# Six matmuls of a row block: by halves of the tokens in place of by weights

## The chip, the cores and the metric

The kernel runs on one core of a Trainium2 chip. The metric is the device time of one execution in microseconds, as the median of several runs. TensorE multiplies, ScalarE, VectorE and GpSimd work beside it, and SP issues most of the DMAs.

## What is computed

Two layers of a streaming encoder, for 512 prompt tokens and 32 sample tokens with shared weights (544 tokens, 1024 features). All of it is float32. Cut to what matters here, each layer is

```python
# even layer: gated DeltaNet heads and forgetting attention; odd layer: sliding-window attention
xp = xp + ab_mixer(rmsnorm(xp, g_mix), ...)          # or c_mixer
mk, mv = mem_kv(mem_prompt, g_mem, w_xkv)            # 256 memory tokens @ w_xkv
xp = xp + cross_attend(rmsnorm(xp, g_cross), mk, mv, w_xq, w_xo)
xp = xp + sq_relu_mlp(rmsnorm(xp, g_mlp), w_up, w_down)

def sq_relu_mlp(h, w_up, w_down):
    return jnp.square(jax.nn.relu(h @ w_up)) @ w_down   # 1024 -> 4096 -> 1024
```

and the same for xs. Nearly all the arithmetic lies in the products of a 1024-row input with a weight matrix: the input projections, the output projections, the queries and keys of the cross-attention, and above all the two MLPs.

## The kernel before

**Products in two parts.** Every factor of a large product is split into a high part and a low part that TensorE reads as fp32r: the weights into wh (ScalarE's copy, line 1588) and wl (GpSimd's difference, line 722), the activations into xh and xl (or hh and hl in the MLP, mh and ml for the memory tokens, y_split for the output of the first layer's heads). A product is the sum of three: wh with the high part, wh with the low part, wl with the high part.

**Tiles.** A product works through its weights in panels of 256 columns (2048 numbers in each partition), alternately in slot 0 and slot 1 of stage, wh and wl. A panel gives two tiles of 128 output features. A tile needs eight blocks, one for each 128 rows of the weights (k, "row block"); in the product behind the cross-attention, with 512 input rows, a panel has four tiles of four blocks. The 544 tokens are moved in two halves of 272, TOKENS, since a bank of PSUM holds 512 numbers in a partition. The tensor LP has four banks, and the tiles take them by turns: one fills banks 0 and 1 (half 0, half 1), the next banks 2 and 3. These pairs are the slots that block's first argument names. So a block is six matmuls: three pairs of parts, two halves.

**Order.** The function block (line 826) issues one block, and the loop at line 829 runs over the three pairs of parts outside and over the halves inside; line 831 is the matmul. pair (line 836) calls it for two panels. Where the input is only just being made, pair interleaves the first two tiles and waits ahead of each block: ready(i) for the activations' low part, low_ready for the quarter of wl that the block needs (line 852). The first matmul of a tile waits for the slot to be free (wait_free). The last matmul of a tile raises product_done. Then one instruction of ScalarE or VectorE reads both halves of the slot: relu at line 2005 or the scaled copy at line 2539 in the MLP.

**Products with another order.** The memory product uses the same block with a single half of 256 tokens (halves=((0, MEM),), line 1383 and line 1391), so it writes three matmuls in a row into one bank. In the first layer's output projection, head_parts (line 1327) adds four row blocks of the heads' part to one half at a time, without block: twelve matmuls in a row into one bank, line 1336. The gates' small product at line 1056 has a loop of its own over the parts and the halves.

Of the kernel before, what the change touches and what calls it, by code (L numbers as in the profile page):

```python
# [5 lines left out]
def build_program(nc, t):  # L6
# [44 lines left out]
    p = q = d = 0  # L51
    DRAINED = {}
    for name, panels, tpp in order:
# [3 lines left out]
        p, q, d = p + panels, q + panels * tpp, d + panels * tpp // (2 if name[:3] == "mlp" else 1)  # L57
# [21 lines left out]
    with ctx:  # L79
# [6 lines left out]
        def place(name, shape, dt=f32, at=None):  # L86
            size = 4
            for n in shape[1:]:
                size *= n
            size = (size + 31) // 32 * 32  # L90
            if at is None:
                at = cursor[0]
                cursor[0] += size
            return nc.alloc_sbuf_tensor_at(name, shape, dt, offset=at)
# [8 lines left out]
        wh = [place(f"wh{s}", [128, 2048], f32r) for s in range(2)]  # L103
        wl = [place(f"wl{s}", [128, 2048], f32r) for s in range(2)]
# [718 lines left out]
        def _(pe):  # L823
            TOKENS = ((0, HALF), (HALF, N))

            def block(slot, s, col, k, first, last, kt, halves, X):

                for n_, (w, part) in enumerate(((wh, 0), (wh, 1), (wl, 0))):
                    weights = w[s][:, :].rearrange("p (k n) -> p k n", k=kt)[:, k, col:col + 128]
                    for half, (a, b) in enumerate(halves):  # L830
                        mm = pe.matmul(LP[:, 2 * slot + half, 0:b - a], weights, X[part][k][:, a:b],  # L831
                                       start=(first and n_ == 0), stop=(last and n_ == 2), skip_group_check=True)
                if last:
                    mm.then_inc(product_done, 1)

            def pair(free, Pn, tpp, kt, halves, X, ready, after_first=None, order=None, between=None, halved=False):
# [9 lines left out]
                for s in range(2):  # L846
                    if s and between is not None:
                        between()
                    def low_ready(ks):

                        if not (s == 0 and halved):
                            pe.wait_ge(w_lo, PIECES * (Pn + s) + max(ks) * PIECES // kt + 1)

                    per = max(kt // PIECES, 1)
                    if s == 0 and ready is not None:
                        wait_free(0)
                        for i in range(kt + LAG):
                            if i < kt:
                                ready(i)
                                if i % per == 0:  # L860
                                    low_ready(order[i:i + per])
                                block(0, s, 0, order[i], i == 0, i == kt - 1, kt, halves, X)
                            if i == kt and after_first is not None:
                                after_first()
                            if i == LAG:
                                wait_free(1)
                            if i >= LAG:
                                block(1, s, 128, order[i - LAG], i == LAG, i == kt + LAG - 1, kt, halves, X)
                    for i in range(2 if s == 0 and ready is not None else 0, tpp):
                        tile_n = s * tpp + i  # L870
                        wait_free(tile_n)
                        for k in range(kt):
                            if i == 0 and k % per == 0:
                                low_ready((k,))
                            block(tile_n % 2, s, 128 * i, k, k == 0, k == kt - 1, kt, halves, X)
# [294 lines left out]
            for P, part, at in SUMS:  # L1170
                n_ = H * (part.stop - part.start)
# [1538 lines left out]
```

## Time and profile before

| | |
|---|---|
| median of 3 runs | 1610.47 us (1607.56 to 1611.96) |
| the profiled execution's own time | 1612.56 us |
| its span, first to last instruction | 1609.7 us |
| mean granted TensorE clock | 0.991 |
| TensorE matmul busy | 1568.6 us (97%), 13488 matmuls |
| TensorE weight load busy | 1511.5 us (94%), 13488 loads |
| VectorE / ScalarE / GpSimd busy | 653.1 / 567.3 / 617.1 us |

Busy time is the union of the instructions' times; matmuls overlap one another and the loads, so a row's mean duration is longer than the spacing from one start to the next. The spacing is read from the starts in the timeline.

### The profile page before, as it was taken

The numbers are of one execution on the slowest core, as the hardware profiler recorded it, in microseconds if no ns is written. First come the engines' busy times: TensorE is split into PE (matmuls) and PEld (weight loads), VectorE is DVE, ScalarE is ACT, GpSimd is POOL, SyncE is SP. The second block draws the span as 40 slices with busy tenths as digits, with TensorE's granted clock in tenths as the row PEclk, the third lists the DMA queues.
The fourth block names the chain that finished last, engine by engine and source line by source line (L and its number), as shares of the span: only waits on it lengthen the run. The fifth ranks groups of instructions, "written<-read, shape, count | busy, mean of one in ns | idle before, by whom it ended". The sixth has DMA issues, their size and how long they took to land.

```text
span 1609.7 us, 31744 instructions
## 1 busy us (share of the span) xinstructions
PE 1568.6 (97%) x13488; PEld 1511.5 (94%) x13488; DVE 653.1 (41%) x1224; ACT 567.3 (35%) x999; POOL 617.1 (38%) x513
## 2 busy tenths in 40 slices
PE   8999998999999999999999999999999999999998
PEld 8999977888998999999999998699899999999998
DVE  4484156344434522322223534844254223232244
ACT  5123254334435521312223413844354222131332
POOL 3754201113561353453444442035423444443441
PEclk9999999989999999999999999999999999999999
DMA  5222211003241222222223224013412322223221
GB/s 152 92 79 82 80 55 60 3 2 118 84 158 48 80 79 93 91 79 89 96 79 99 86 79 146 2 54 105 131 31 82 99 79 95 90 79 105 79 79 56
DMA packets 123060, 131.84 MB, mean 82 GB/s; under 512 B 6285, under 2 KB 115122, under 8 KB 122930
## 3 DMA queue, kind: packets, MB, share of 16 engines
q1 hardware_dynamic: 118128, 125.24, 24.2%
q10 hardware_dynamic: 4802, 4.66, 0.9%
q8 instruction: 106, 1.74, 0.4%
q14 instruction: 24, 0.20, 0.0%
HBM read 122.44 MB, written 7.45 MB: 81 GB/s over the span
## 4 chain that ended last, share of the span: by engine, by line
PE 46%; issue 31%; POOL 17%; DVE 3%; ACT 2%; DMA 1%; POOLq 0%; ACTq 0%; DVEq 0%
PE LP L831 37%; POOL wl L722 17%; PE LP L1216 3%; PE MP L982 1%; PE LP L934 1%; DMA stage<-in_w_in_ab 1%; PE MP L1056 0%; PE MP L1200 0%; PE MP L1216 0%; PE MP L1303 0%; ACT probs L1641 0%; PE MP L1073 0%; PE MP L1308 0%; PE MP L1312 0%; PE MP L955 0%
## 5 line engine op out<-in xcount | busy, mean ns | idle before, releaser
L722 POOL TENSOR_TENSOR wl<-stage,wh 128x512 fp32r<-128x512 f32 x428 | 576.8, 1379 | 806.2 <-ACT wh L1588 793.7
L831 PE MATMUL LP<-xh,wh 128*128 128x272 f32 x2112 | 441.6, 290 | 8.2 <-DVE xl L2149 5.3
L831 PE MATMUL LP<-xl,wh 128*128 128x272 f32 x2112 | 436.9, 288 | 0.0
L831 PE MATMUL LP<-xh,wl 128*128 128x272 f32 x2112 | 436.5, 288 | 0.0
L1588 ACT CAST wh<-stage 128x2048 fp32r<-128x2048 f32 x107 | 203.7, 1904 | 443.4 <-PE LP L831 418.1
L831 PEld LDWEIGHTS LP<-xh,wh 128*128 128x128 f32 x2112 | 332.1, 189 | 11.4 <-DVE xl L2149 6.9
L831 PEld LDWEIGHTS LP<-xl,wh 128*128 128x128 f32 x2112 | 332.9, 189 | 0.0
L831 PEld LDWEIGHTS LP<-xh,wl 128*128 128x128 f32 x2112 | 331.0, 189 | 0.0
L831 PE MATMUL LP<-hl,wh 128*128 128x272 f32 x1024 | 211.1, 287 | 0.0
L831 PE MATMUL LP<-hh,wh 128*128 128x272 f32 x1024 | 210.6, 287 | 0.0
L831 PE MATMUL LP<-hh,wl 128*128 128x272 f32 x1024 | 210.5, 287 | 0.0
L831 PEld LDWEIGHTS LP<-hh,wl 128*128 128x128 f32 x1024 | 160.7, 188 | 0.0
L831 PEld LDWEIGHTS LP<-hh,wh 128*128 128x128 f32 x1024 | 160.2, 188 | 0.0
L831 PEld LDWEIGHTS LP<-hl,wh 128*128 128x128 f32 x1024 | 160.1, 188 | 0.0
L2524 DVE TENSOR_TENSOR hsq<-rel 128x544 f32<-128x544 f32 x64 | 51.3, 801 | 261.5 <-ACT rel L2005 254.9
L2539 DVE TENSOR_TENSOR dtmp<-LP,rstd 128x544 f32<-128x544 f32 x64 | 46.4, 725 | 245.4 <-PE LP L831 245.4
L2005 ACT ACTIVATE rel<-LP 128x544 f32<-128x544 f32 x64 | 40.0, 625 | 236.9 <-PE LP L831 236.9
L1613 ACT ACTIVATE sq<-x 128x544 f32<-128x544 f32 x56 | 36.6, 654 | 102.7 <-DVE x L2542 56.2
L805 POOL TENSOR_TENSOR BT<-LT,level 128x256 f32<-128x256 f32 (+1 forms) x24 | 18.4, 779 | 138.2 <-DVE LT L2422 104.8
L2528 DVE TENSOR_TENSOR hl<-hsq,hh 128x544 fp32r<-128x544 f32 x64 | 69.7, 1090 | 2.2
L2149 DVE SCALAR_TENSOR_TENSOR xl<-x,cols,xh 128x544 fp32r<-128x544 f32 x48 | 48.5, 1025 | 40.1 <-ACT xh L1618 38.9
L2142 DVE TENSOR_TENSOR acc<-acc,sq 128x544 f32<-128x544 f32 x49 | 47.1, 962 | 16.7 <-ACT sq L1613 14.8
(415 smaller groups left out, 1675.4 us busy)
## 6 DMA issues: line engine op xcount, KB each, us to landing
stage<-in_w_up SPq DMA_DIRECT2D x32, 1024.0 KB, 5.4
stage<-in_w_down SPq DMA_DIRECT2D x32, 1024.0 KB, 5.2
stage<-in_w_in_ab SPq DMA_DIRECT2D x13, 1024.0 KB, 5.3
stage<-in_w_xkv SPq DMA_DIRECT2D x8, 1024.0 KB, 5.2
stage<-in_w_in_c SPq DMA_DIRECT2D x6, 1024.0 KB, 5.0
stage<-in_w_out_ab SPq DMA_DIRECT2D x4, 1024.0 KB, 9.4
stage<-in_w_xq SPq DMA_DIRECT2D x4, 1024.0 KB, 5.3
stage<-in_w_xo SPq DMA_DIRECT2D x4, 1024.0 KB, 5.2
```

The lines of the kernel that those rows point to most:

```text
L722: pool.tensor_tensor(wl[s][:, part], stage[s][:, part], wh[s][:, part].bitcast(f32), ALU.subtract).then_inc(w_lo, 1)
L805: pool.tensor_tensor(BT[s][0:P, k % 2, :, 0:C], LT[s][0:P, :, 0:C], lower, ALU.mult).then_inc(inv_pool[s], 1)
L831: mm = pe.matmul(LP[:, 2 * slot + half, 0:b - a], weights, X[part][k][:, a:b], start=(first and n_ == 0), stop=(last and n_ == 2), skip_gr ...
L1216: return pe.matmul(out, lhsT, rhs, start=start, stop=stop, skip_group_check=True)
L1588: act.copy(wh[s][:, :], stage[s][:, :]).then_inc(w_hi, 1)
L1613: act.activation(sq[:, k % 2, :], x[:, k, :], ACT.Square).then_inc(sq_ready, 1)
L2005: act.activation(rel[:, k % 2, :].rearrange("p (a n) -> p a n", a=2), LP[:, 2 * (k % 2):2 * (k % 2) + 2, 0:HALF], ACT.Relu).then_inc(relu_ ...
L2142: dve.tensor_tensor(acc[:, :], acc[:, :], sq[:, k % 2, :], ALU.add).then_inc(sq_used, 1)
L2149: dve.scalar_tensor_tensor(out=xl[:, k, :], in0=x[:, k, :], scalar=gain(n_, k), in1=xh[:, k, :].bitcast(f32), op0=ALU.mult, op1=ALU.subtra ...
L2524: dve.tensor_tensor(hsq[:, k % 2, :], rel[:, k % 2, :], rel[:, k % 2, :], ALU.mult).then_inc(hsq_ready, 1)
L2528: dve.tensor_tensor(hl[:, k, :], hsq[:, k % 2, :], hh[:, k, :].bitcast(f32), ALU.subtract).then_inc(h_ready, 1)
L2539: dve.tensor_tensor(two(dtmp[:, k % 2, :]), banks(k), two(rstd[:, :]), ALU.mult).then_inc(drained, 1)
```

## The change

The two loops of block change places. Before, the pairs of parts are outside and the halves inside, so consecutive matmuls share their weights and alternate between the two banks of the slot. After, the halves are outside: three matmuls (wh with high, wh with low, wl with high) go into the bank of half 0, and then three into the bank of half 1. The flags start and stop are set by the same conditions, the last matmul of a tile is the same, and no wait is moved.

```diff
             def block(slot, s, col, k, first, last, kt, halves, X):
 
-                for n_, (w, part) in enumerate(((wh, 0), (wh, 1), (wl, 0))):
-                    weights = w[s][:, :].rearrange("p (k n) -> p k n", k=kt)[:, k, col:col + 128]
-                    for half, (a, b) in enumerate(halves):
+                for half, (a, b) in enumerate(halves):
+                    for n_, (w, part) in enumerate(((wh, 0), (wh, 1), (wl, 0))):
+                        weights = w[s][:, :].rearrange("p (k n) -> p k n", k=kt)[:, k, col:col + 128]
                         mm = pe.matmul(LP[:, 2 * slot + half, 0:b - a], weights, X[part][k][:, a:b],
                                        start=(first and n_ == 0), stop=(last and n_ == 2), skip_group_check=True)
                 if last:
```

## Rows read from the trace of the kernel before

**Rows 1.** The page: span; busy time, share, instructions; shares of the chain by engine.

```profile
span 1609.7 us, 31744 instructions
...
PE 1568.6 (97%) x13488; PEld 1511.5 (94%) x13488; DVE 653.1 (41%) x1224; ACT 567.3 (35%) x999; POOL 617.1 (38%) x513
...
PE 46%; issue 31%; POOL 17%; DVE 3%; ACT 2%; DMA 1%; POOLq 0%; ACTq 0%; DVEq 0%
```

**Rows 2.** The longest piece of the chain that ended last: start us, us, what.

```profile
1220.68 375.61 PE LP L831 x3006
```

**Rows 3.** Waits of TensorE: who waited for whom, us in total, times, longest us.

```profile
PE LP L831 <- DVE xl L2149: 5.3, 6, 2.1
PE LP L831 <- POOL wl L722: 3.1, 7, 0.9
```

**Rows 4.** Groups by line and operation: shapes, xcount, busy us, mean ns, idle before.

```profile
L831 PE MATMUL LP<-xh,wh 128*128 128x272 f32 x2112 | 441.6, 290 | 8.2 <-DVE xl L2149 5.3 <-DVE xl L2219 1.8 <-POOL wl L722 0.9
...
L831 PE MATMUL LP<-hh,wl 128*128 128x272 f32 x1024 | 210.5, 287 | 0.0
...
L831 PEld LDWEIGHTS LP<-xh,wh 128*128 128x128 f32 x2112 | 332.1, 189 | 11.4 <-DVE xl L2149 6.9 <-DVE xl L2219 2.2 <-POOL wl L722 1.1
...
L831 PE MATMUL LP<-y_split,wh 128*128 128x272 f32 x96 | 16.1, 290 | 0.0
...
L831 PE MATMUL LP<-mh,wh 128*128 128x256 f32 x128 | 37.0, 289 | 3.0 <-POOL wl L722 2.2 <-DVE kvT L2495 0.8
...
L831 PE MATMUL LP<-y_split,wl 128*128 128x272 f32 x48 | 9.9, 288 | 0.0
```

**Rows 5.** Timeline of TensorE, 391 to 398 us: start us, us, engine, line, names, shapes, xcount.

```profile
391.77 0.29 PE L1336 MATMUL LP<-y_split,wl 128*128 128x272 f32 x1
...
394.42 0.29 PE L1336 MATMUL LP<-y_split,wl 128*128 128x272 f32 x1
394.54 0.66 PE L831 MATMUL LP<-y_split,wh 128*128 128x272 f32 x4
395.05 0.41 PE L831 MATMUL LP<-y_split,wl 128*128 128x272 f32 x2
...
397.32 0.42 PE L831 MATMUL LP<-y_split,wl 128*128 128x272 f32 x2
```

**Rows 6.** Timeline of TensorE, memory product of the second layer, first and last rows of 46.

```profile
1119.14 0.28 PE L831 MATMUL LP<-mh,wl 128*128 128x256 f32 x1
1119.26 0.28 PE L831 MATMUL LP<-mh,wh 128*128 128x256 f32 x1
...
1124.46 0.27 PE L831 MATMUL LP<-mh,wl 128*128 128x256 f32 x1
```

**Rows 7.** Timeline of TensorE in the MLP, first and last rows of 16.

```profile
1495.83 0.41 PE L831 MATMUL LP<-hh,wh 128*128 128x272 f32 x2
1496.08 0.42 PE L831 MATMUL LP<-hl,wh 128*128 128x272 f32 x2
...
1499.58 0.41 PE L831 MATMUL LP<-hh,wh 128*128 128x272 f32 x2
```

**Rows 8.** Stretches of TensorE: us, busy (xcount), granted clock, DMA share, GB/s.

```profile
18.00:30.00 12.00, 11.51 (x84) 0.86 0.20 17
130.00:200.00 70.00, 69.25 (x557) 0.98 0.25 77
260.00:340.00 80.00, 75.60 (x1251) 0.89 0.10 31
600.00:1600.00 1000.00, 989.60 (x8043) 1.00 0.26 82
1118.00:1125.00 7.00, 6.74 (x58) 1.00 0.60 197
```

**Rows 9.** The page's costliest groups, the readers of the finished tiles in the MLP.

```profile
L2539 DVE TENSOR_TENSOR dtmp<-LP,rstd 128x544 f32<-128x544 f32 x64 | 46.4, 725 | 245.4 <-PE LP L831 245.4
L2005 ACT ACTIVATE rel<-LP 128x544 f32<-128x544 f32 x64 | 40.0, 625 | 236.9 <-PE LP L831 236.9
```

## The prediction

> **What bounds the kernel now.** I read the busy table first: TensorE is busy for 1568.6 us of the 1609.7 us span, and VectorE, ScalarE and GpSimd each for 35% to 41% [rows 1]. So the matmuls set the time, unless their 97% hides waiting. The chain that ended last says that it does not: its longest piece is a single run of 3006 matmuls of line 831, 375.61 us long, without a wait in between [rows 2]. That is 375.61 / 3006 = 124.95 ns from one matmul to the next. By engine the chain names GpSimd for 17% and "issue" for 31% [rows 1], but these are places where the program follows another engine back although TensorE is not idle; the table of TensorE's own waits decides, and it holds little: the two longest entries of line 831 are 5.3 us for the low halves of x and 3.1 us for the low parts of the weights [rows 3].
>
> What is edited is line 831 itself. By the counts of its groups it has 2112 matmuls of each of three kinds on x (xh with wh, xl with wh, xh with wl), 1024 of each of three kinds on h, and 96 and 48 on y_split, each of 272 columns; the rows show one kind of each [rows 4]. That is 3 x 2112 + 3 x 1024 + 144 = 9552 matmuls, or 1592 blocks of six. At 125.0 ns these are 1194 us, three quarters of the span. The matmuls on the memory tokens (128 of each of three kinds, 256 columns) have one half only, so their order stays as it is. Everything hangs on one number: does the 125.0 ns from start to start change when the same six matmuls come in another order?
>
> **What the change does to the order.** Before, one block writes the banks as a b a b a b, with the weights wh wh wh wh wl wl and the tokens of xh, xh, xl, xl, xh, xh. After, it writes a a a b b b, with the weights wh wh wl wh wh wl. Nothing is added or taken away: six matmuls, six weight loads, the same operands, and within each bank the same three sums in the same order. Two things per block differ. First, of six steps from matmul to matmul all six changed the bank, and now two do; four steps in six, 4 x 1592 = 6368 in all, now stay in the bank that the matmul before wrote. Second, of six steps three changed the weights, and now four do, which is 1592 more.
>
> **Step 1: the cost of staying in a bank.** The trace of before has both orders side by side, with one operand (y_split) and one width (272 columns). Line 1336 writes three in a row into one bank, and stays there for four row blocks, twelve matmuls, before it goes to the next bank. The matmuls with wl in its rows start at 391.77 and 394.42 us, and seven triples lie between them [rows 5]: 2.65 us / 21 = 126.2 ns. Directly behind, line 831 works on the same operand with the banks in turn: from 395.05 to 397.32 us there are three blocks, 2.27 us / 18 = 126.1 ns. The stamps have steps of 10 ns, so each mean is good to about 0.5 ns, and the difference is +0.1 ns with bounds of about -0.7 and +0.7. The second witness is the memory product, on the same line 831, three in a row into one bank. From 1119.14 to 1124.46 us there are fifteen triples [rows 6]: 5.32 us / 45 = 118.2 ns at 256 columns. In the MLP, with the banks in turn, 30 matmuls of 272 columns take 1495.83 to 1499.58 us [rows 7]: 125.0 ns. The granted clock is 1.00 at both places [rows 8], the level of 2.4 GHz, so 16 columns less should be 16 / 2.4 = 6.7 ns less, and 125.0 - 6.7 = 118.3 ns. Measured 118.2. Put otherwise, what a matmul takes beyond its columns is 125.0 - 113.3 = 11.7 ns with the banks in turn and 118.2 - 106.7 = 11.5 ns three in a row. So I take 0 ns for a step that stays in its bank, and as bounds -0.2 and +0.1 ns from the two comparisons' own differences: 6368 x (-0.2) = -1.3 us and 6368 x 0.1 = +0.6 us. With the rounding of the stamps in full (0.7 ns) the outer bounds would be -4.5 and +4.5 us.
>
> **Step 2: the cost of changing the weights more often.** Every matmul already has a weight load of its own: the two columns of the busy table both count 13488 [rows 1], and the groups of line 831 have as many loads as matmuls [rows 4]. A load takes 189 ns and a matmul 288 ns, while matmuls start every 125 ns, so loads and matmuls overlap. Could the load of the same weights a second time be cheaper? The memory product changes its weights at two steps in three, as the new order does, against one in two before, and its surplus is 11.5 ns against 11.7. The two differ by one change in six steps, so a change would be priced at 6 x (11.5 - 11.7) = -1.2 ns, with some 1.8 ns either way from the stamps: nothing that can be told from 0. I take 0 for the 1592 further changes, with +0.6 ns each (+1.0 us) and -1.2 ns each (-1.9 us) as bounds. Here the Trainium skill has a rule that speaks against the change: the page "TensorE: Matmul & The Clock Gate", section "Step-by-step: what each phase is for", says that loads and matmuls are separate instructions so that weights can be loaded once and used for many matmuls. By that rule the old order has the better shape, and each further change would cost. In this kernel nothing is loaded once: the trace counts one load for each matmul, and the sum would differ by the bound just given at most.
>
> **Step 3: waits and readers.** The waits for xl (through ready) and for the low weights (low_ready, line 852) stand ahead of a whole block. That wl is now needed by the third matmul and not by the fifth, and xl by the second and not the third, delays nothing. The semaphore of a finished tile still rides on the last matmul, half 1 with wl. Half 0 is complete two matmuls, or 250 ns, earlier than before, but no one can use it: the readers take both halves in one instruction, 128x544 [rows 9]. No wait is added, the queues of SP, GpSimd, ScalarE and VectorE keep their order, and their release times stay. Cost 0 on both sides.
>
> **Sum.** 1609.7 us span + 0 + 0 + 0 = 1609.7 us, and with the 2.9 us around it the profiled execution's 1612.6 us. That execution lies 2.1 us above the median of the runs, 1610.47. I therefore predict 1610.5 us.
>
> **The rivals.**
>
> *Faster: changing the bank costs something.* Of the 125.0 ns, 11.7 are not columns. Were all of that the price of a bank change, 6368 steps would give back 74.5 us, and the kernel would take 1536 us. The memory product speaks against it: with no bank change it has the same surplus. What is left is a small share that the stamps hide. At 1 ns a step it would be -6.4 us, 1604.1 us. It decides from 0.76 ns a step, since 0.3% is 4.8 us and 4.8 / 6368 = 0.76 ns.
>
> *Faster: the clock.* Before 370 us the granted clock drops in places: 0.86 from 18 to 30 us, 0.98 from 130 to 200 us, 0.89 between 260 and 340 us [rows 8]. Only the first two stretches are full of line 831. If turn and turn about of the banks made the clock drop there, the change would bring back 0.14 x 12 + 0.02 x 70 = 3.1 us, 1607.4 us, still within 0.3%. But line 831 runs in the same order at 1.00 from 600 to 1600 us, so the order is not what lowers it. The Trainium skill has that rule, too: in "TensorE: Matmul & The Clock Gate", section "A second HAM failure mode: psum-queue depth-cycling", cycling through the PSUM banks is said to make TensorE pause so often that its clock swings between the two levels. By that rule this kernel should swing all along; the trace does not agree, with 1.00 for a thousand us.
>
> *Slower: a sum has to wait for the one before it in its bank.* A matmul lasts 288 ns by its record and the next starts after 125 ns, so in the new order up to three matmuls on the same addresses are under way at once. If the second had to wait for the first to end, the spacing would be 288 ns on four steps in six: 6368 x 163 ns = 1038 us, 2650 us in all. Line 1336 and the memory product do just this and show nothing of it, so the full price is excluded. What they can't exclude is a small stall that needs something they lack, such as ScalarE and VectorE reading the other two banks at the same time, all along. At 1.5 ns a step: +9.6 us, 1620.1 us. It decides from 0.76 ns a step on, that is, where the mean of a long run rises above 125.5 ns (0.76 x 4 / 6).
>
> **How the numbers follow.** No change, 0.90: 1610.5 us, with the range 1606 to 1615 from the bounds of steps 1 and 2 and the runs of before, which lie between 1607.56 and 1611.96 us. Faster by a bank change's price, 0.04: about 1604. The clock, 0.02: 1607.4, within 0.3%. Slower by a stall in the bank, 0.04: about 1620. The range reaches to the first of the faster cases and part of the way to the slower one: 1604 to 1616. About 0.3% is what a measurement of this kernel can tell from no change; so faster 0.04, within 0.3% 0.92, slower 0.04.
>
> **What would show it.** In the profile of after: 13488 loads and 13488 matmuls; in the MLP, twelve matmuls of line 831 in 1.50 us, as now; the memory product at 118 ns, since it is untouched; the readers' 128x544 at their old durations; TensorE busy for about 1569 us, its waits of the same size and at the same places; the granted clock at 1.00 from 600 to 1600 us. The prediction is wrong if the long piece of line 831 has a mean outside 124.5 to 125.5 ns, if fewer weight loads appear (then repeated weights are dealt with in a way that this trace does not show), or if the waits for ScalarE, VectorE or GpSimd grow, which I expect from no step.

## The result and the profile after

The median goes from 1610.47 us (five runs, 1604.11 to 1611.96) to 1619.29 us (five runs, 1617.06 to 1621.49). The ratio is 1.0063, with a 95% interval from 1.0043 to 1.0084. The kernel is slower: the two medians differ by 8.8 us, and the ratio stands for 10 us. The profiled execution took 1618.84 us, with a span of 1616.7 us against 1609.7 us before.

The page's span, busy times and shares of the chain, which answer to [rows 1]:

```profile
span 1616.7 us, 31744 instructions
...
PE 1572.7 (97%) x13488; PEld 1515.6 (94%) x13488; DVE 653.1 (40%) x1224; ACT 567.4 (35%) x999; POOL 614.9 (38%) x513
...
PE 46%; issue 31%; POOL 17%; DVE 3%; ACT 2%; DMA 1%; ACTq 0%; POOLq 0%; DVEq 0%
```

Same counts of matmuls and loads, same shares of the chain. What moved is the long piece of the chain (start us, us, what), which answers to [rows 2]:

```profile
1223.13 378.99 PE LP L831 x3006
```

The same 3006 matmuls of line 831 take 378.99 us in place of 375.61: 126.08 ns from one to the next, not 124.95. This is +1.12 ns, and if all 9552 edited matmuls rose like these, 10.7 us. They do not quite. Taking the mean of all steps below 200 ns in the two traces, x blocks outside the MLPs (blocks whose tokens are xh and xl) go from 125.3 to 126.1 ns, x blocks in the MLPs from 125.1 to 126.1 and h blocks (on hh and hl) from 124.8 to 126.0, which makes 9.5 us. The rest is nearly as it was. TensorE's waits, to be held against [rows 3], and the groups, against [rows 4] and [rows 9]:

```profile
PE LP L831 <- DVE xl L2149: 6.6, 7, 2.2
PE LP L831 <- POOL wl L722: 3.2, 7, 0.9
```

```profile
L831 PE MATMUL LP<-xh,wh 128*128 128x272 f32 x2112 | 614.5, 291 | 9.4 <-DVE xl L2149 6.6
...
L831 PEld LDWEIGHTS LP<-xh,wh 128*128 128x128 f32 x2112 | 398.6, 189 | 12.6 <-DVE xl L2149 8.4
...
L2539 DVE TENSOR_TENSOR dtmp<-LP,rstd 128x544 f32<-128x544 f32 x64 | 46.4, 725 | 247.0 <-PE LP L831 247.0
L2005 ACT ACTIVATE rel<-LP 128x544 f32<-128x544 f32 x64 | 40.0, 626 | 239.7 <-PE LP L831 239.7
```

The waits for xl and wl grew by 1.3 and 0.1 us. The duration of one matmul (290 ns before, 291 after), of one load and of the two readers did not move. The busy total of the matmul groups rises from 441.6 to 614.5 us, but that is only how the union is counted: before, two matmuls of one kind followed each other and overlapped, now each kind stands alone. That column says nothing of speed here, only the spacing does.

TensorE's stretches (us, busy and count, granted clock, DMA share, GB/s), which answer to [rows 8]:

```profile
18.00:30.00 12.00, 10.26 (x83) 1.00 0.20 19
...
260.00:340.00 80.00, 75.60 (x1292) 0.91 0.10 32
600.00:1600.00 1000.00, 990.51 (x7988) 1.00 0.26 82
```

In this execution the clock was lower for less of the time than in that of before: 1.00 from 18 to 30 us in place of 0.86, 0.91 between 260 and 340 us in place of 0.89, and a mean of 0.995 against 0.991. Counted at full speed, 0.9% of 1610 us (14.5 us) were lost before and 0.5% of 1617 us (8.1 us) after. The spans differ by 7.0 us, 2.5 us less than the 9.5 us that the edited matmuls cost more; the clock's 6.4 us are an upper bound of what it gave back, and cover that.

The two rows on which my forecast rested, again after the change. First line 831 on y_split, against [rows 5]:

```profile
392.79 0.29 PE L831 MATMUL LP<-y_split,wl 128*128 128x272 f32 x1
...
395.45 0.29 PE L831 MATMUL LP<-y_split,wl 128*128 128x272 f32 x1
```

From the first to the last of these there are seven triples: 2.66 us / 21 = 126.7 ns, against 126.1 before. Then the memory product, against [rows 6]; its order is untouched:

```profile
1124.68 0.28 PE L831 MATMUL LP<-mh,wl 128*128 128x256 f32 x1
...
1126.45 0.28 PE L831 MATMUL LP<-mh,wl 128*128 128x256 f32 x1
```

Five triples, 1.77 us / 15 = 118.0 ns, as before within the stamps.

### The profile page after: what moved, and what is told of

It reads as the page before. It is cut to its first block, busy times and chain, and to the rows that moved or that the text cites. A ratio compares the mean times of both kernels' runs of the same rounds, so it can differ in the third digit from the quotient of the medians.

```text
span 1616.7 us, 31744 instructions
## 1 busy us (share of the span) xinstructions
PE 1572.7 (97%) x13488; PEld 1515.6 (94%) x13488; DVE 653.1 (40%) x1224; ACT 567.4 (35%) x999; POOL 614.9 (38%) x513
## 4 chain that ended last, share of the span: by engine, by line
PE 46%; issue 31%; POOL 17%; DVE 3%; ACT 2%; DMA 1%; ACTq 0%; POOLq 0%; DVEq 0%
PE LP L831 37%; POOL wl L722 17%; PE LP L1216 3%; PE MP L982 1%; PE LP L934 1%; DMA stage<-in_w_in_ab 1%; PE MP L1056 0%; PE MP L1216 0%; PE MP L1200 0%; PE MP L1303 0%; PE MP L1192 0%; ACT probs L1641 0%; PE MP L1073 0%; PE MP L1308 0%; PE MP L955 0%
## 5 line engine op out<-in xcount | busy, mean ns | idle before, releaser
L831 PE MATMUL LP<-xh,wh 128*128 128x272 f32 x2112 | 614.5, 291 | 9.4 <-DVE xl L2149 6.6
L831 PE MATMUL LP<-xl,wh 128*128 128x272 f32 x2112 | 611.0, 289 | 0.0
L831 PE MATMUL LP<-xh,wl 128*128 128x272 f32 x2112 | 610.8, 289 | 0.0
L831 PEld LDWEIGHTS LP<-xh,wh 128*128 128x128 f32 x2112 | 398.6, 189 | 12.6 <-DVE xl L2149 8.4
L831 PEld LDWEIGHTS LP<-xl,wh 128*128 128x128 f32 x2112 | 398.0, 188 | 0.2
L831 PEld LDWEIGHTS LP<-xh,wl 128*128 128x128 f32 x2112 | 398.1, 189 | 0.0
L831 PE MATMUL LP<-hh,wh 128*128 128x272 f32 x1024 | 296.5, 290 | 0.0
L831 PE MATMUL LP<-hh,wl 128*128 128x272 f32 x1024 | 296.3, 289 | 0.0
L831 PE MATMUL LP<-hl,wh 128*128 128x272 f32 x1024 | 294.8, 288 | 0.0
L831 PEld LDWEIGHTS LP<-hl,wh 128*128 128x128 f32 x1024 | 193.0, 188 | 0.0
```

## The experiments

**How spacing is read below.** There are two measures, both good to a few hundredths of a ns. The long piece of the chain, 3006 matmuls, mixes x blocks and h blocks. To part the two I take starts from the timeline of TensorE: the first matmul of an x product in the second layer's MLP, the first of the h product behind it, and the first of the next x product. 384 matmuls lie between each two. For the kernel before, these are the starts and those of the next two products:

```profile
1308.40 0.29 PE L831 MATMUL LP<-xh,wh 128*128 128x272 f32 x1
...
1356.40 0.29 PE L831 MATMUL LP<-hh,wh 128*128 128x272 f32 x1
...
1404.19 0.28 PE L831 MATMUL LP<-xh,wh 128*128 128x272 f32 x1
...
1452.30 0.29 PE L831 MATMUL LP<-hh,wh 128*128 128x272 f32 x1
...
1500.33 0.29 PE L831 MATMUL LP<-xh,wh 128*128 128x272 f32 x1
```

The first x product takes 48.00 us / 384 = 125.0 ns and the first h product 47.79 us / 384 = 124.5 ns. But the next x product takes 48.11 us, 125.3 ns, and the next h product 48.03 us, 125.1 ns. Read like this over the MLPs of both layers, the x products of before stand at 125.0 or 125.3 ns (mean 125.1), and the h products at 125.1 and 124.5 ns by turns (mean 124.8), and e1_bank and e2_weights repeat this product by product. The placement and the order are the same in all of them, so something else switches between these levels; no run shows what. In each of the other kernels the x products of the MLPs agree within 0.02 ns and the h products within 0.06 ns, so there one product of each kind speaks for the MLPs. It does not speak for the x blocks outside them, as will be seen. For the kernel after:

```profile
1311.47 0.29 PE L831 MATMUL LP<-xh,wh 128*128 128x272 f32 x1
...
1359.89 0.28 PE L831 MATMUL LP<-hh,wh 128*128 128x272 f32 x1
...
1408.30 0.29 PE L831 MATMUL LP<-xh,wh 128*128 128x272 f32 x1
```

48.42 and 48.41 us: 126.1 ns in both. (The expectations below quote 125.1 and 124.8 ns for before. These are its means over both levels, and they are the values to compare with.) Each ratio below is against runs of the kernel before taken beside that experiment.

**Which of three orders is it?** The edit changes three orders at once: of the banks, of the weights and of the tokens' reads. Four kernels take them apart. In all experiments but e9_weights_64 and e10_tokens_64 block goes through a list of six entries (weights, high or low part, half of the tokens, bank); for the memory product it is a list of three, in the old order (left out here):

```diff
-                for n_, (w, part) in enumerate(((wh, 0), (wh, 1), (wl, 0))):
-                    weights = ...
-                    for half, (a, b) in enumerate(halves):
-                        mm = pe.matmul(LP[:, 2 * slot + half, 0:b - a], weights, X[part][k][:, a:b], ...
+                seq = ((wh, 0, 0, 0), (wh, 0, 1, 1), (wh, 1, 0, 0), (wh, 1, 1, 1), (wl, 0, 0, 0), (wl, 0, 1, 1))
+                for n_, (w, part, half, bank) in enumerate(seq):
+                    ...
+                    a, b = halves[half]
+                    mm = pe.matmul(LP[:, 2 * slot + bank, 0:b - a], weights, X[part][k][:, a:b], ...
```

The list shown is that of before; start and stop go to the first and last use of a bank. The diffs between lists below are against this one. e1_bank only changes the fourth column:

```diff
-                seq = ((wh, 0, 0, 0), (wh, 0, 1, 1), (wh, 1, 0, 0), (wh, 1, 1, 1), (wl, 0, 0, 0), (wl, 0, 1, 1))
+                seq = ((wh, 0, 0, 0), (wh, 0, 1, 0), (wh, 1, 0, 0), (wh, 1, 1, 1), (wl, 0, 0, 1), (wl, 0, 1, 1))
```

> A block's six matmuls keep the weights and the tokens of before, in the order of before, and write the banks in the order of after (a a a b b b). Sums of different tokens meet in one bank, so the products are not the reference's; only the time is read. Theory 1 (a step that stays in its bank costs some 1.7 ns, four steps in six): spacing in the long run of line 831 126.1 ns as after, ratio about 1.006. Theory 2 (the two further changes of weights per block cost 3.4 ns each) and theory 3 (a matmul whose tokens lie directly behind those of the one before is cheaper): 125.0 ns as before, ratio 1.000.

Measured: 1610.37 us, ratio 1.0004 (0.9986 to 1.0023). Its long piece:

```profile
1213.80 375.61 PE LP L834 x3006
```

375.61 us, to the hundredth as before. e2_weights changes only the first column:

```diff
-                seq = ((wh, 0, 0, 0), (wh, 0, 1, 1), (wh, 1, 0, 0), (wh, 1, 1, 1), (wl, 0, 0, 0), (wl, 0, 1, 1))
+                seq = ((wh, 0, 0, 0), (wh, 0, 1, 1), (wl, 1, 0, 0), (wh, 1, 1, 1), (wh, 0, 0, 0), (wl, 0, 1, 1))
```

> The tokens and banks are in the order of before, the weights in the order of after (wh wh wl wh wh wl). So wl meets xl and other wrong pairs; only the time is read. Theory 1 (bank) and theory 3 (tokens): spacing 125.0 ns, ratio 1.000. Theory 2 (a change of weights costs): four changes in six in place of two, spacing 126.1 ns, ratio about 1.006.

Measured: 1607.86 us, ratio 1.0000 (0.9988 to 1.0012), and once more 375.61 us:

```profile
1213.11 375.61 PE LP L834 x3006
```

e3_tokens changes only the second and third columns:

```diff
-                seq = ((wh, 0, 0, 0), (wh, 0, 1, 1), (wh, 1, 0, 0), (wh, 1, 1, 1), (wl, 0, 0, 0), (wl, 0, 1, 1))
+                seq = ((wh, 0, 0, 0), (wh, 1, 0, 1), (wh, 0, 0, 0), (wh, 0, 1, 1), (wl, 1, 1, 0), (wl, 0, 1, 1))
```

> The weights and banks are in the order of before, the tokens in the order of after (xh a, xl a, xh a, xh b, xl b, xh b). So the banks hold wrong sums; only the time is read. Theory 1 (bank) and theory 2 (weights): spacing 125.0 ns, ratio 1.000. Theory 3 (before, the second matmul of each pair reads on where the first ended; that is lost in this order): spacing 126.1 ns, ratio about 1.006.

Measured: 1618.07 us, ratio 1.0064 (1.0041 to 1.0087). The long piece is that of after:

```profile
1221.65 378.99 PE LP L834 x3006
```

e4_all_but_bank is the counter-test: weights and tokens as after, banks by turns.

```diff
-                seq = ((wh, 0, 0, 0), (wh, 0, 1, 1), (wh, 1, 0, 0), (wh, 1, 1, 1), (wl, 0, 0, 0), (wl, 0, 1, 1))
+                seq = ((wh, 0, 0, 0), (wh, 1, 0, 1), (wl, 0, 0, 0), (wh, 0, 1, 1), (wh, 1, 1, 0), (wl, 0, 1, 1))
```

> The weights and the tokens are in the order of after, the banks still by turns as before. The sums in the banks are wrong; only the time is read. Theory 1 (bank): spacing 125.0 ns, ratio 1.000. Theories 2 and 3: 126.1 ns, ratio about 1.006.

Measured: 1619.27 us, ratio 1.0061 (1.0038 to 1.0083):

```profile
1224.65 378.99 PE LP L834 x3006
```

This settles the first question. The loss comes with the order in which the tokens are read, and all of it does: 378.99 us with that order and 375.61 us without, whatever the banks and the weights do. Staying in a bank costs nothing, and neither do the further changes of weights.

**What in the order of the reads?** Two simple theories were left: reading on where the last matmul ended is cheaper (3a), or going to another tensor costs (3b). In e5_second_half_first the second half goes first in each pair; nothing reads on any more, and the tensors change as seldom as before.

```diff
-                seq = ((wh, 0, 0, 0), (wh, 0, 1, 1), (wh, 1, 0, 0), (wh, 1, 1, 1), (wl, 0, 0, 0), (wl, 0, 1, 1))
+                seq = ((wh, 0, 1, 1), (wh, 0, 0, 0), (wh, 1, 1, 1), (wh, 1, 0, 0), (wl, 0, 1, 1), (wl, 0, 0, 0))
```

> The kernel of before, but in each pair the second half of the tokens goes first (b a b a b a). The products are the same and complete. Same weights order, same banks by turns, and the tokens change from xh to xl and back as seldom as before; what is lost is that a matmul reads on where the one before it ended (four steps in six before, none here). Theory 3a (reading on is cheaper): spacing at least 126.1 ns, by four steps lost against the two that after loses 127.2 ns, ratio 1.006 to 1.013. Theory 3b (going from one activation tensor to another costs, two steps in six before and four after): 125.0 ns, ratio 1.000.

Measured: 1618.88 us, ratio 1.0071 (1.0043 to 1.0099). Its three starts:

```profile
1309.80 0.29 PE L834 MATMUL LP<-xh,wh 128*128 128x272 f32 x1
...
1358.60 0.29 PE L834 MATMUL LP<-hh,wh 128*128 128x272 f32 x1
...
1406.23 0.29 PE L834 MATMUL LP<-xh,wh 128*128 128x272 f32 x1
```

x blocks: 48.80 us, 127.1 ns. h blocks: 47.63 us, 124.0 ns. The total looks like theory 3a, but against the means of before one kind got slower by 2.0 ns and the other faster by 0.7 ns with the same edit, and neither theory allows that. What parts x blocks from h blocks is where their rows lie. Counted from where the kernel's first buffer starts, a row of xh or xl starts at a multiple of 128 bytes in its partition, a row of hh or hl 64 bytes beyond one; rows are 2176 = 17 x 128 bytes apart, and the second half starts 1088 = 8.5 x 128 bytes behind the first. So an x block alternates between starts at 0 and 64 (modulo 128), and an h block between 64 and 0. Two kernels take the alternation away.

In e6_same_tokens all six matmuls of a block read the same columns:

```diff
-                seq = ((wh, 0, 0, 0), (wh, 0, 1, 1), (wh, 1, 0, 0), (wh, 1, 1, 1), (wl, 0, 0, 0), (wl, 0, 1, 1))
+                seq = ((wh, 0, 0, 0), (wh, 0, 0, 1), (wh, 0, 0, 0), (wh, 0, 0, 1), (wl, 0, 0, 0), (wl, 0, 0, 1))
```

> All six matmuls of a block read the same 272 columns, the first half of the high part; weights and banks in the order of before. Five matmuls' worth of other tokens are left out; only the time is read. No step goes to another tensor within a block, and none reads on. Theory 3a (reading on is cheaper): spacing above 125.0 ns, about 127.2. Theory 3b (change of tensor costs): below 125.0 ns, about 123.9.

Measured in a single execution: 1615.24 us.

```profile
1309.88 0.29 PE L834 MATMUL LP<-xh,wh 128*128 128x272 f32 x1
...
1358.31 0.29 PE L834 MATMUL LP<-hh,wh 128*128 128x272 f32 x1
...
1406.31 0.29 PE L834 MATMUL LP<-xh,wh 128*128 128x272 f32 x1
```

x blocks: 48.43 us, 126.1 ns. h blocks: 48.00 us, 125.0 ns. e7_shift_before and e8_shift_after read six different pieces, but let the second half start at a multiple of 128 bytes behind the first, in the order of before and of after:

```diff
+                halves = ((0, 272), (256, 528)) if len(halves) == 2 else halves
```

> Order of before, but the second half reads columns 256 to 528 in place of 272 to 544: as wide as before, but it starts at 1024 bytes behind the first half's start, a multiple of 128, and no longer at 1088. The last 16 tokens' product is left out and 16 others are computed twice; only the time is read. Theory 3a (reading on is cheaper): nothing reads on any more, spacing 126 to 127 ns. Theory 3c (a start between two lines of 128 bytes costs, less so when the line was just read): 125.0 ns or less. Theory 3b: 125.0 ns.

> Order of after, the second half reads columns 256 to 528 (as in e7_shift_before). Theory 3a (reading on is cheaper): 126.1 ns or a little more, since one more step loses it. Theory 3b (change of tensor costs): 126.1 ns. Theory 3c (a start between two lines of 128 bytes costs): as e7_shift_before, 125.0 ns or less.

Measured: e7 1614.59 us, ratio 1.0037 (1.0017 to 1.0057); e8 1612.65 us, ratio 1.0021 (1.0008 to 1.0035). Their intervals overlap, and the long pieces are equal, e7 first:

```profile
1217.27 377.25 PE LP L835 x3006
```

```profile
1223.13 377.25 PE LP L835 x3006
```

377.25 us in both, and in e6 too: 125.5 ns in the mean. So when all six reads start alike modulo 128 bytes, neither their order nor reading on nor the change of tensors matters any more; what is left in the MLPs is a difference by kind, 126.1 ns for x blocks (starts at 0) and 125.0 ns for h blocks (starts at 64). Theories 3a and 3b are refuted by this. Theory 3c is right that the starts matter, and wrong that starts at multiples of 128 are the cheap ones: it expected 125.0 ns or less for both kernels.

**The start by itself, or against the weights?** e9_weights_64 moves the weights' buffers by 64 bytes and leaves xh, xl, hh and hl where they are, with the order of before. stage, which stands ahead of them, and the buffers behind them up to the old place of the two small tensors (rstd, acc, sq and constants) move along, in the later placements too; no run parts these from the weights.

```diff
+        eps_col = place("eps_col", [128, 1])
+        one_col = place("one_col", [128, 1])
         stage_at = cursor[0]
...
-        eps_col = place("eps_col", [128, 1])
-        one_col = place("one_col", [128, 1])
```

> Order of before. Only the place of wh, wl and stage in SBUF moves by 64 bytes (two small tensors of 32 bytes stand ahead of them); xh, xl, hh and hl stay. So far, blocks on xh/xl (starts at multiples of 128 bytes) take 125.1 ns a matmul in the order of before, and blocks on hh/hl (64 beyond a multiple of 128) 124.8. Theory A (only the tokens' addresses and their order count): both stay, the run of 3006 keeps 375.6 us, ratio 1.000. Theory R (what counts is how the tokens' addresses lie against those of the weights that are loaded at the same time): both change by some tenths of a ns to 1 ns, the run of 3006 shifts by over 1 us.

Measured: 1610.30 us, ratio 1.0002 (0.9990 to 1.0014). The total hides that both kinds of blocks moved:

```profile
1301.66 0.29 PE L831 MATMUL LP<-xh,wh 128*128 128x272 f32 x1
...
1349.45 0.29 PE L831 MATMUL LP<-hh,wh 128*128 128x272 f32 x1
...
1397.56 0.29 PE L831 MATMUL LP<-xh,wh 128*128 128x272 f32 x1
```

x blocks 47.79 us (124.5 ns, before 125.0 or 125.3), h blocks 48.11 us (125.3 ns, before 124.5 or 125.1). Both values lie outside the levels of before, although the tokens did not move, so their address alone does not set the spacing. Theory R also wanted the long piece to shift by over 1 us, and this it missed: 375.75 us against 375.61, since the two kinds moved against each other. e12_same_tokens_weights_64 asks the same with the alternation taken away; it is e6_same_tokens with the placement of e9_weights_64.

> As e6_same_tokens (all six matmuls of a block read the first half of the high part; other products left out, only the time is read), with wh and wl moved by 64 bytes as in e9_weights_64. In e6_same_tokens blocks on xh took 126.0 ns and blocks on hh 125.0. Theory A (the tokens' start alone): the same again, 126.0 and 125.0. Theory R (the tokens' start against the weights' start): the two change places, 125.0 for xh and 126.0 for hh.

Measured in a single execution: 1608.38 us.

```profile
1303.98 0.29 PE L834 MATMUL LP<-xh,wh 128*128 128x272 f32 x1
...
1351.98 0.29 PE L834 MATMUL LP<-hh,wh 128*128 128x272 f32 x1
...
1400.20 0.29 PE L834 MATMUL LP<-xh,wh 128*128 128x272 f32 x1
```

x blocks fell from 126.1 to 125.0 ns, just to the value that h blocks had, as theory R wants. h blocks rose from 125.0 to 125.6, not to 126.1. e16_second_first_weights_64 asks it where the differences are largest: the list of e5_second_half_first with the placement of e9_weights_64.

> Halves by turns with the second half first, as in e5_second_half_first, all products complete; wh and wl moved by 64 bytes as in e9_weights_64, the tokens' buffers where they were. In e5_second_half_first one product on xh/xl took 127.1 ns a matmul and one on hh/hl 124.05. Theory A (the tokens' start alone): the same again. Theory R (the tokens' start against the weights' start): xh/xl now lie against the weights as hh/hl did and fall to 124.05 ns, while hh/hl rise, at most to 127.1; if hh/hl stay under 125.5 the kernel is faster than before, ratio 0.992 to 0.998, else 0.998 to 1.002.

Measured: 1607.11 us, ratio 0.9989 (0.9977 to 1.0000).

```profile
1301.02 0.28 PE L834 MATMUL LP<-xh,wh 128*128 128x272 f32 x1
...
1348.61 0.29 PE L834 MATMUL LP<-hh,wh 128*128 128x272 f32 x1
...
1397.40 0.28 PE L834 MATMUL LP<-xh,wh 128*128 128x272 f32 x1
```

x blocks 47.59 us, 123.9 ns; h blocks 48.79 us, 127.1 ns. In e5 it was 127.1 and 124.0. They changed places, with the tokens where they were and the weights moved by 64 bytes. Theory A is refuted.

e10_tokens_64 moves xh and xl by 64 bytes and the weights by 128, in the order of before, so that x rows lie against the weights, modulo 128, as h rows do:

```diff
+        eps_col = place("eps_col", [128, 1])
+        one_col = place("one_col", [128, 1])
         xh_at = cursor[0]
...
+        mem_ss = place("mem_ss", [128, 2])
+        mem_rs = place("mem_rs", [128, 2])
         stage_at = cursor[0]
...
-        eps_col = place("eps_col", [128, 1])
-        one_col = place("one_col", [128, 1])
...
-        mem_ss = place("mem_ss", [128, 2])
-        mem_rs = place("mem_rs", [128, 2])
```

> Order of before. Only xh and xl move by 64 bytes (and the weights by 128), so that their rows start where those of hh and hl do, 64 beyond a multiple of 128. Theory A (start of the tokens against lines of 128 bytes, and order): blocks on xh/xl take what those on hh/hl take, 124.8 ns in place of 125.1, the run of 3006 shortens by some 0.5 us to 375.1 us, ratio 0.999 to 1.000. Theory C (which tensor, and what else the other engines read and write in that stage, makes the difference between x and h): 375.6 us as before.

Measured: 1610.38 us, ratio 1.0003 (0.9991 to 1.0016). It missed both theories of its expectation by a little, since the long piece grew:

```profile
1217.97 376.03 PE LP L831 x3006
```

376.03 us. x and h blocks now take the same, 125.0 and 125.1 ns, where the h products of before took 125.1 and 124.5 ns by turns. The h rows did not move and the weights moved by just 128 bytes, and yet none of the eight h products is at 124.5 ns any more. Since before itself goes from one level to the other with every address in place, this alone does not say that the address matters beyond its place modulo 128. The memory product of the same trace does. Its tokens, mh and ml, did not move either, nor did its order change:

```profile
1116.42 0.28 PE L831 MATMUL LP<-mh,wl 128*128 128x256 f32 x1
...
1121.81 0.28 PE L831 MATMUL LP<-mh,wl 128*128 128x256 f32 x1
```

Fifteen triples, 5.39 us / 45 = 119.8 ns, where before took 5.32 us / 45 = 118.2 ns [rows 6], both at a granted clock of 1.00. The traces of e11 and e14, in the same placement, show this rise as well. So a shift of the weights by a whole 128 bytes, with the buffers behind them, changes the spacing by 1.6 ns there: the place modulo 128 bytes is not all.

**Is the loss tied to this layout?** (Layout is the same as placement: where the buffers start.) e13_after_weights_64 and e14_after_tokens_64 run the order of after in the placements of e9 and e10.

> The order of after, with wh and wl moved by 64 bytes. If the loss belongs to the order: 126.0 to 126.1 ns in both kinds of blocks as in after, run of 3006 379.0 us, ratio 1.006. If it belongs to how the addresses of this layout lie (theory R): another value, for which 125.5 ns (the mean of 126.0 and 125.0) is as likely as any, ratio 1.000 to 1.006.

> The order of after, with xh and xl moved by 64 bytes and the weights by 128 as in e10_tokens_64, where the order of before took 125.1 ns. If the loss belongs to the order: 126.0 to 126.1 ns, run of 3006 379.0 us, ratio 1.006. If to the layout: another value.

Measured: e13 1620.32 us, ratio 1.0068 (1.0046 to 1.0090); e14 1617.75 us, ratio 1.0058 (1.0034 to 1.0082). Long pieces, e13 first:

```profile
1231.94 378.99 PE LP L834 x3006
```

```profile
1224.64 378.99 PE LP L834 x3006
```

378.99 us, the same as after, in all three placements. In the MLPs the loss belongs to the order, as far as these placements go: where the order of before takes 124.5 to 125.3 ns, three reads in a row from each half take 126.0 to 126.1. Outside the MLPs it depends on the placement. The longest run there, 576 matmuls of the first product, is one piece of the chain (start us, us, what), here of before, e9, e10 and after:

```profile
55.41 72.16 PE LP L831 x576
54.96 71.68 PE LP L831 x576
54.90 72.63 PE LP L831 x576
55.39 72.64 PE LP L831 x576
```

These are 125.3, 124.4, 126.1 and 126.1 ns. In the placement of e10 the order of before is as slow here as that of after, although in the MLP of the same execution its x blocks take 125.0 ns. So the halves by turns give different levels from one product to another, and a level read in one product can't be carried to the next. e15_after_second_first starts that order from the other half (b b b a a a), in the placement of before.

```diff
-                seq = ((wh, 0, 0, 0), (wh, 1, 0, 0), (wl, 0, 0, 0), (wh, 0, 1, 1), (wh, 1, 1, 1), (wl, 0, 1, 1))
+                seq = ((wh, 0, 1, 1), (wh, 1, 1, 1), (wl, 0, 1, 1), (wh, 0, 0, 0), (wh, 1, 0, 0), (wl, 0, 0, 0))
```

> The layout of before, the order of after from the other half: b b b a a a, all products complete. In the alternating order, starting with the second half made 127.1 of 125.1 ns on xh/xl and 124.1 of 124.8 on hh/hl. If it is the phase of each half against the weights that counts, xh/xl and hh/hl part here too, by 1 ns or more, around 125.5 or 126.1. If three in a row even that out: both at 126.1 ns as in after, ratio 1.006.

Measured: 1616.71 us, ratio 1.0045 (1.0027 to 1.0063).

```profile
1220.72 378.34 PE LP L834 x3006
```

378.34 us: by the starts of its products 126.1 ns in x blocks and 125.6 in h blocks, so three in a row even out most of what the first half to be read makes in the order by turns, though not all of it.

**A version that beats both.** Halves by turns with the second half first was quick where the tokens lay 64 bytes off the weights (e5's h blocks, e16's x blocks). e11_tokens_64_second_first gives x blocks and h blocks that place: the placement of e10 and the list of e5.

> xh and xl moved by 64 bytes as in e10_tokens_64, and in each pair the second half of the tokens first, as in e5_second_half_first, where blocks on hh/hl took 124.1 ns and blocks on xh/xl 127.1. All products complete. Theory A: now both take 124.1 ns, the run of 3006 takes 372.9 us, and the kernel is faster than before by 9552 x 0.9 ns, some 9 us: ratio 0.994 to 0.995. Theory C: blocks on xh/xl stay at 127.1 ns, ratio about 1.006.

Measured: 1597.43 us, ratio 0.9919 (0.9902 to 0.9936), with all products computed. It is faster than before by 0.8%; after, measured beside other runs of before, is 0.6% slower than before.

```profile
1295.66 0.29 PE L834 MATMUL LP<-xh,wh 128*128 128x272 f32 x1
...
1343.25 0.29 PE L834 MATMUL LP<-hh,wh 128*128 128x272 f32 x1
...
1390.87 0.29 PE L834 MATMUL LP<-xh,wh 128*128 128x272 f32 x1
```

```profile
1208.77 372.70 PE LP L834 x3006
```

47.59 and 47.62 us: 123.9 and 124.0 ns. The long piece is 2.91 us shorter than before, 0.97 ns a matmul, which makes 9.3 us over 9552; by the mean steps of all blocks in the trace it is 9.7 us. The medians differ by 12.5 us, more than the 9 us expected. The other 3 us I can't place with certainty; the mean granted clock of these runs was 0.9952 against 0.9937 of the runs of before beside them, worth 2.4 us at most. Against e10, with the same placement, only the order of the halves differs: 125.0 and 125.1 became 123.9 and 124.0 ns. That theory A named the right number here is no support for it; e16 refutes it, and theory R gives the same number.

The spacings together, in ns, from the starts of one x product and one h product (e7, e8, e10 and e13 to e15 by the same reading), and with both levels where products of one kind differ. In the order, a is the first half of the tokens and b the second. "Weights" and "rows" are starts modulo 128 bytes, counted from the first buffer.

| kernel | order of the halves | weights | x rows | h rows | x blocks | h blocks |
|---|---|---|---|---|---|---|
| before, e1, e2 | a b a b a b | 0 | 0 | 64 | 125.0 or 125.3 | 124.5 or 125.1 |
| e9 | a b a b a b | 64 | 0 | 64 | 124.5 | 125.3 |
| e10 | a b a b a b | 0 | 64 | 64 | 125.0 | 125.1 |
| e5 | b a b a b a | 0 | 0 | 64 | 127.1 | 124.0 |
| e16 | b a b a b a | 64 | 0 | 64 | 123.9 | 127.1 |
| e11 | b a b a b a | 0 | 64 | 64 | 123.9 | 124.0 |
| after, e3, e4 | a a a b b b | 0 | 0 | 64 | 126.1 | 126.1 |
| e13 | a a a b b b | 64 | 0 | 64 | 126.1 | 126.1 |
| e14 | a a a b b b | 0 | 64 | 64 | 126.1 | 126.1 |
| e15 | b b b a a a | 0 | 0 | 64 | 126.1 | 125.6 |
| e6, e7, e8 | all starts alike | 0 | 0 | 64 | 126.1 | 125.0 |
| e12 | all starts alike | 64 | 0 | 64 | 125.0 | 125.6 |

## Why the prediction was wrong

I forecast no change, 1610.5 us with a range of 1604 to 1616, and gave slower a chance of 0.04. It became 1619.3 us.

**What failed is the list that steps 1 and 2 rest on.** It says that two things per block differ, the banks and the weights. The edit changes a third, the order in which the tokens are read, and the sum has no term for it: it was put at nothing without a reason, although the sentences ahead of the list had written the sequence down. That term is the whole loss. e3_tokens, with this order alone, takes 378.99 us for the long piece, as after does, against 375.61: +1.12 ns for each of its matmuls, and 9.5 to 10.7 us over the 9552 edited ones. Step 1 took 0 ns for the new order because staying in a bank costs 0 ns, which e1_bank and e4_all_but_bank bear out. Its bounds, 4.5 us at the outermost, were bounds for the bank alone.

**The rows held a warning.** Line 1336, which runs in the order of after, stood at 126.2 ns [rows 5], and the MLP at 125.0 [rows 7], with the same width and the same clock. That the 1.1 ns between them is just the loss that came is luck: line 831 on y_split took 126.1 with the halves by turns as well, and in the trace of after it rose only to 126.7 in the stretch shown and to 126.4 in the mean. But a control on the same operand that is itself 1.1 ns slower than the body of the kernel proves nothing about the body; the gap between [rows 5] and [rows 7] was as large as the effect looked for and needed an explanation of its own. y_split is not laid out like the others: its rows are 550 numbers, 2200 bytes, apart and not 2176, so its starts fall on many places modulo 128. That the row pitch (the distance from row to row) is what makes y_split slow in both orders is argued from the other kernels, not shown: no run changed the pitch.

**The second witness did not bear on it either.** The memory product moves one piece of 256 columns from each row, rows a multiple of 128 bytes apart, so all its reads start alike modulo 128, and e7 and e8 show that then the order was without effect. And comparing 118.2 with 125.0 ns through 16 columns assumed a fixed surplus over the columns. It isn't fixed: by the same subtraction, at 272 columns it goes from 123.9 - 113.3 = 10.6 ns (e11) to 127.1 - 113.3 = 13.8 ns (e5, x blocks). In the memory product itself it goes from 11.5 ns to 119.8 - 106.7 = 13.1 ns in e10. That 11.5 and 11.7 ns agreed was luck of the placement.

**Step 2 was right in its result and wrong in a count.** Before, the weights change at two steps in six and not at three (wh stays for four matmuls), so the change adds two for each block, 3184 and not 1592, and the comparison with the memory product would have priced one change at half of the -1.2 ns. e2_weights shows that they cost nothing: its long piece is 375.61 us, and its trace still counts one load for each matmul. The rule of loading once and multiplying often (the Trainium skill, "TensorE: Matmul & The Clock Gate", "Step-by-step: what each phase is for"), taken as the prediction took it, would have made e2 slower; its ratio is 1.0000 (0.9988 to 1.0012).

**Step 3 held.** Loads and matmuls are 13488 each, the readers take 725 and 626 ns, and the two longest waits of TensorE grew by 1.3 and 0.1 us.

**The rivals.** The slower rival came out in size, 1620.1 us against 1619.3, and at the point that it named: the long run's mean rose above 125.5 ns. That is luck. Its mechanism, a sum that waits for the one before in its bank, is refuted by e1_bank, which has the same banks as after and the time of before. The faster rival by the price of a bank change is refuted by the same run. The clock took no part in the difference between the orders: the long piece lies where it stands at 1.00 in both [rows 8].

**The range** was built from the bounds of the question asked. The spread of the spacing over the kernel's own rows, 125.0 to 126.2 ns at one width, would have given 9552 x 1.2 ns = 11.5 us upwards, and a range up to 1622 us. It holds the result.

## What to carry to other kernels

When an edit permutes instructions, write down the order of every operand (weights, moved columns, destination), cost each, and look in the trace for a row that runs in the new order with the same row pitch and start; if two rows of one shape differ by a percent, that is a cause not yet understood and belongs in the range. Where matmuls run back to back for most of the span, 1 ns in 125 is 0.8% of that part: try the order of the halves and a shift of the buffers by 64 bytes, for both together gave 0.8% here while each alone gave nothing or a loss. Read spacing from starts far apart, not from busy sums, which went from 441.6 to 614.5 us for the same work, and read more than one product of a kind: in the kernel before, two neighbours differed by 0.6 ns.

## What the runs showed of the hardware

At 272 columns and a granted clock of 1.00, the spacing of back-to-back matmuls with a load each lay between 123.9 and 127.1 ns in the MLPs' products, and repeated to 0.01 us over 3006 matmuls between kernels that read the tokens in the same order in the same placement (375.61 us in before, e1 and e2, 378.99 us in after, e3 and e4). It depends on the order in which the tokens' columns are read and on where they start against the weights: moving the weights, and the buffers behind them, by 64 bytes made x blocks and h blocks change places at 127.1 and 123.9 to 124.0 ns (e5, e16). It did not depend on whether consecutive matmuls write the same bank (375.61 us in e1), nor on whether the weights change twice or four times in six (375.61 us in e2). One guess is that the reads of the tokens and the loads of the next weights get in each other's way, since both run at the same time; no run shows that. Two things stay open. One is by which part of the address it goes: the place modulo 128 bytes explains the exchange in e16, but not e10, where a shift of the weights by a whole 128 bytes moved the memory product from 118.2 to 119.8 ns. The other is what sets the level of a product when the halves go by turns: h products in the kernel before take 125.1 and 124.5 ns by turns, with the same order and the same addresses, and in e10 x blocks take 126.1 ns in the first product and 125.0 ns in the MLPs.
